# The second gate unit as twelve-bit parts, with the embedding's products moved between the two gate units

## What is computed

```python
x = layer_norm(ALPHA * x + mix, ln2_g[i], ln2_b[i])
ple = jax.nn.sigmoid(x @ w_ple_gate[i]) * (p[i] @ w_ple[i])
x = layer_norm(ALPHA * x + 0.5 * swiglu(x, ffn2_up[i], ffn2_down[i]) + ple, ln3_g[i], ln3_b[i])
```

## Time and profile before

| | |
|---|---|
| median of 3 runs | 2663.27 us (2658.33 to 2663.58) |
| profiled execution, its own time | 2664.31 us |
| span of it | 2662.6 us |
| mean granted TensorE clock | 0.997 |
| PE busy | 2624.8 us, 99% |
| DVE busy | 1116.0 us, 42% |
| ACT busy | 676.8 us, 25% |

### The profile page before, as it was taken

How to read it: one execution, slowest core, us unless ns; L and a number is a source line. 1 busy time by engine, 2 the same in 40 slices (tenths; PEclk the granted TensorE clock), 3 DMA queues, 4 the chain that set the end, 5 groups by cost and what they waited for, 6 DMA issues and landing times.

```text
span 2662.6 us, 38037 instructions
## 1 busy us (share of the span) xinstructions
PE 2624.8 (99%) x15353; PEld 1916.1 (72%) x15353; DVE 1116.0 (42%) x1589; ACT 676.8 (25%) x1202; POOL 73.4 (3%) x95
## 2 busy tenths in 40 slices
PE   8999999999999999999999999999999999999998
PEld 8989888999999998899989888843333333333333
DVE  6866424586587563157832143321212112112212
ACT  3414220342143042213412043021212121112111
POOL 0010200000000120000001000000000000000000
PEclk9999999999999999999999999999999999999999
DMA  7575334356655843334562644689999999999999
GB/s 240 189 271 182 125 127 164 137 177 221 234 176 186 293 166 117 136 143 159 173 215 90 225 151 158 248 352 427 428 427 428 428 428 428 427 427 427 427 427 411
DMA packets 265217, 705.27 MB, mean 265 GB/s; under 512 B 13076, under 2 KB 155360, under 8 KB 215072
## 3 DMA queue, kind: packets, MB, share of 16 engines
q1 hardware_dynamic: 253520, 663.66, 64.7%
q0 software_dynamic: 9856, 36.41, 3.8%
q10 hardware_dynamic: 1744, 3.83, 0.5%
HBM read 699.61 MB, written 6.60 MB: 265 GB/s over the span
## 4 chain that ended last, share of the span: by engine, by line
PE 82%; DMA 9%; SPq 8%; issue 1%; DVE 1%; ACT 0%; DVEq 0%
PE acc L989 12%; PE acc L1086 11%; PE acc L1708 9%; PE acc L1043 6%; PE mix L1047 6%; PE acc L1045 6%; SPq L871 5%; PE acc L1723 4%; PE acc L1528 4%; PE mix L1037 4%; PE acc L1015 3%; DMA big<-in_w 3%; SPq L874 2%; PE acc L1320 2%; DMA ring<-in_w 2%; DMA zp<-in_w 2%
## 5 line engine op out<-in xcount | busy, mean ns | idle before, releaser
L1043 PE MATMUL acc<-branch_parts,area_parts 128*128 128x256 f32 x1176 | 345.1, 293 | 4.4 <-DVE zz_parts L2360 4.3
L1047 PE MATMUL mix<-big_parts,zz_parts 128*128 128x256 f32 x1176 | 333.7, 284 | 0.0
L1045 PE MATMUL acc<-area_parts,ring_parts 128*128 128x256 f32 x1176 | 333.4, 284 | 0.0
L1086 PE MATMUL acc<-big,ring 128*128 128x256 f32 (+1 forms) x1408 | 269.7, 353 | 0.0
L1086 PEld LDWEIGHTS acc<-big,ring 128*128 128x128 f32 x1408 | 241.1, 190 | 28.3 <-issue 0.8
L3018 DVE COPY zz<-acc 128x512 f32<-128x512 f32 x32 | 22.1, 691 | 548.9 <-PE acc L1708 548.9
L1043 PEld LDWEIGHTS acc<-branch_parts,area_parts 128*128 128x128 f32 x1176 | 226.0, 192 | 13.6 <-DVE zz_parts L2360 5.2
L1045 PEld LDWEIGHTS acc<-area_parts,ring_parts 128*128 128x128 f32 x1176 | 226.1, 192 | 0.2
L1047 PEld LDWEIGHTS mix<-big_parts,zz_parts 128*128 128x128 f32 x1176 | 226.0, 192 | 0.0
L989 PE MATMUL acc<-x,ring 128*128 128x256 f32 x1024 | 224.3, 380 | 0.0
L989 PEld LDWEIGHTS acc<-x,ring 128*128 128x128 f32 x1024 | 193.8, 190 | 26.7 <-issue 0.3
(11 more groups left out here) (519 smaller groups left out, 3813.8 us busy)
## 6 DMA issues: line engine op xcount, KB each, us to landing
big<-in_w SPq DMA_DIRECT2D x89, 1024.0 KB, 25.9
ring<-in_ffn_up SPq DMA_DIRECT2D x86, 1024.0 KB, 5.0
ring<-in_w SPq DMA_DIRECT2D x84, 1024.0 KB, 25.9
ring<-in_w_in SPq DMA_DIRECT2D x72, 1024.0 KB, 7.1
spare<-in_w SPq DMA_DIRECT2D x42, 1024.0 KB, 25.9
area<-in_w_ada POOLq DMA_DIRECT2D x24, 1024.0 KB, 8.5
tables<-in_w SPq DMA_DIRECT2D x23, 1024.0 KB, 25.9
branch<-in_w SPq DMA_DIRECT2D x23, 1024.0 KB, 25.4
```

Source lines behind the costliest of these rows:

```text
L1043: pe.matmul(abank(a, b)[:, ts], wg[:, b, k, c * P:c * P + P], xg[:, k, :], start=c == 0 and k == 0, stop=False, skip_group_check=True)
L1045: pe.matmul(abank(a, b)[:, ts], wl[:, k, c0:c0 + P], xl[:, k, :], start=False, stop=k == K - 1, skip_group_check=True)
L1047: mm = pe.matmul(kbank(a, b)[:, ts], wk[:, b, k, c * P:c * P + P], xk[:, k, :], start=False, stop=k == K - 1, skip_group_check=True)
L1086: mm = pe.matmul(outs[c], w[:, k, c * P:c * P + P], rhs(kk), start=opens[c] and kk == 0, stop=kk == FC - 1, skip_group_check=not all(opens))
```

## The change

The second gate unit is multiplied by parts and not in the plain way, and is moved behind the embedding's products. It is counted as unit -1 of the second feed-forward (`split_unit(1, -1)`). The groups are renumbered: PLEG 39, PLE 40 and 41, the second gate unit (`G_PLEG_1`) 42. The embedding's second group is first copied into `res` by DVE and multiplied by the sigmoid later, as one instruction of 1024 elements.

```diff
             def split_product(L, s, u, i=0):
-                if s == 2:
+                whole = s == 2 or u == -1
+                if whole:
                     unit_landed(pe, L, r)
...
                 product_halves(L, PLEG, G_PLEG, cols, 32, between=lambda: half_stats(L, 1, 1, 4, 8))
-                product(L, PLEG + 1, G_PLEG + 1, xs, cols)
                 pe.wait_ge(apart_landed, (L + 1) * 48)
                 for hf in range(2):
                     a = G_PLE + hf
...
+                split_product(L, 1, -1)
                 ffn(L, UP2, G_UP2, 2)
```

On ACT:

```diff
-                for n in range(2):
-                    a = G_PLEG + n
-                    for b in range(2):
-                        bank_done(act, L, a, b)
-                        g = act.activation(big[:, 4 * n + 2 * b:4 * n + 2 * b + 2, :],
-                                           abank(a, b).rearrange("p (c t) -> p c t", c=2), ACT.Sigmoid)
-                    g.then_inc(acc_free[a % 2], 1)
-                    act.drain().then_inc(ple_gate, 1)
-                    if n == 0:
-                        for hf in range(2):
-                            upper(L, 1, 0, hf)
+                for hf in range(2):
+                    upper(L, 1, -1, hf)
+                a = G_PLEG
+                for b in range(2):
+                    bank_done(act, L, a, b)
+                    g = act.activation(big[:, 2 * b:2 * b + 2, :], abank(a, b).rearrange("p (c t) -> p c t", c=2), ACT.Sigmoid)
+                g.then_inc(acc_free[a % 2], 1)
+                act.drain().then_inc(ple_gate, 1)
+                a = G_PLEG_1
+                for b in range(2):
+                    bank_done(act, L, a, b)
+                    copy(big[:, 4 + 2 * b:6 + 2 * b, :], kbank(a, b).rearrange("p (c t) -> p c t", c=2)).then_inc(k_summed, 1)
+                    upper(L, 1, 0, b)
+                for b in range(2):
+                    act.wait_ge(a_joined, 26 * L + 13 + b + 1)
+                    act.activation(big[:, 4 + 2 * b:6 + 2 * b, :], big[:, 4 + 2 * b:6 + 2 * b, :], ACT.Sigmoid)
+                act.drain().then_inc(ple_gate, 1)
```

On DVE:

```diff
                 for hf in range(2):
-                    lower(L, 1, 0, hf)
+                    lower(L, 1, -1, hf)
+                v.wait_ge(ple_gate, L * 2 + 1)
                 for n in range(2):
                     a = G_PLE + n
-                    v.wait_ge(ple_gate, L * 2 + (n + 1))
                     for b in range(2):
                         bank_done(v, L, a, b)
                         m = 4 * n + 2 * b
-                        o = tt(res[:, m:m + 2, :], pair(abank(a, b)), big[:, m:m + 2, :], ALU.mult)
+                        o = tt(res[:, m:m + 2, :], pair(abank(a, b)), big[:, m:m + 2, :], ALU.mult) if n == 0 else \
+                            v.tensor_copy(res[:, m:m + 2, :], pair(abank(a, b)))
                     o.then_inc(acc_free[a % 2], 1)
+                for b in range(2):
+                    o = join(L, 1, -1, b, big[:, 4 + 2 * b:6 + 2 * b, :])
+                    if b:
+                        o.then_inc(acc_free[G_PLEG_1 % 2], 1)
+                    v.drain().then_inc(a_joined, 1)
+                    lower(L, 1, 0, b)
+                v.wait_ge(ple_gate, L * 2 + 2)
+                tt(res[:, 4:8, :], res[:, 4:8, :], big[:, 4:8, :], ALU.mult)
                 v.drain()
                 v.scalar_tensor_tensor(out=res[:, :, :], in0=res[:, :, :], scalar=1 / ALPHA, in1=x[:, :, :],
                                        op0=ALU.mult, op1=ALU.add)
```

More of the change, by code:

```diff
@@ L42 @@
 UP1, DOWN1, PROJ, GATE, MERGE, WOUT, PLEG, PLE, UP2, DOWN2, UNITS = 0, 11, 19, 24, 32, 34, 36, 38, 39, 50, 58
-G_UP1, G_DOWN1, G_PROJ, G_GATE, G_MERGE, G_WOUT, G_PLEG, G_PLE, G_UP2, G_DOWN2, GROUPS = \
-    0, 11, 15, 21, 29, 37, 39, 41, 43, 54, 58
+G_UP1, G_DOWN1, G_PROJ, G_GATE, G_MERGE, G_WOUT, G_PLEG, G_PLE, G_PLEG_1, G_UP2, G_DOWN2, GROUPS = \
+    0, 11, 15, 21, 29, 37, 39, 40, 42, 43, 54, 58
 ORDER = (0, 2, 3, 1)
@@ L675, in parts_made @@
         def parts_made(L, s):
-            return 56 * L + (0, 32, 22)[s]
+            return 58 * L + (0, 32, 22)[s]
         def half_parts(L, s, n, b):
-            return parts_made(L, s) + (2 * n + b + 3 if s == 1 else 2 * n + b + 1)
+            return parts_made(L, s) + (2 * n + b + 5 if s == 1 else 2 * n + b + 1)
         def sums_made(L, s):
-            return 50 * L + (0, 28, 20)[s]
+            return 52 * L + (0, 28, 20)[s]
         UPS = ((UP1, G_UP1), (UP2, G_UP2))
         def split_unit(s, n):
+            if (s, n) == (1, -1):
+                return PLEG + 1
             return UPS[s][0] + n if s < 2 else (PROJ + n if n < 4 else GATE)
         def split_group(s, n):
+            if (s, n) == (1, -1):
+                return G_PLEG_1
             return UPS[s][1] + n if s < 2 else (G_PROJ + n if n < 4 else G_GATE)
@@ L1028, in split_product @@
                 w, wl = (m[:, turn_of(L, r) % 2, :].rearrange("p (k c) -> p k c", c=UC) for m in (ring, ring_parts))
-                if s == 2:
+                whole = s == 2 or u == -1
+                if whole:
                     unit_landed(pe, L, r)
                 for b in range(2):
-                    if s < 2:
+                    if not whole:
                         half_landed(pe, L, r, b, i)
@@ L1856, in upper @@
             def upper(L, s, n, hf):
-                if s == 2:
+                if s == 2 or n == -1:
                     unit_landed(act, L, split_unit(s, n))
@@ L1892, in silus @@
                         upper(L, s, n + 1, 0)
-                    act.wait_ge(a_joined, 24 * L + (13 + n + 1 if s else n))
+                    act.wait_ge(a_joined, 26 * L + (15 + n + 1 if s else n))
                     act.activation(silu[:, a % 2], joined[0], ACT.Silu).then_inc(silu_ready, 1)
@@ L1969, in _ @@
                 k_sum(2, 1, rg)
-                act.wait_ge(a_joined, 24 * L + 10 + 1)
+                act.wait_ge(a_joined, 26 * L + 10 + 1)
                 act.activation(rg, rg, ACT.Silu)
@@ L1981, in _ @@
                 for b in range(2):
-                    act.wait_ge(a_joined, 24 * L + 11 + b + 1)
+                    act.wait_ge(a_joined, 26 * L + 11 + b + 1)
                     act.activation(big[:, 2 * b:2 * b + 2, :], big[:, 2 * b:2 * b + 2, :], ACT.Sigmoid)
@@ L2379, in join @@
                 bank_done(v, L, a, b)
-                v.wait_ge(k_summed, sums_made(L, s) + (2 * n + b + 1 if s == 1 else 2 * n + b - 1))
+                v.wait_ge(k_summed, sums_made(L, s) + (2 * n + b + 3 if s == 1 else 2 * n + b - 1))
                 return v.scalar_tensor_tensor(out=dst, in0=abank(a, b).rearrange("p (c t) -> p c t", c=2), scalar=1.0 + 1.0 / STEP,
```

## The result

The changed kernel took 2670.48 us (median of 7 runs, 2669.60 to 2675.28), the kernel before in the same rounds 2661.58 us (7 runs, 2658.33 to 2663.58). The ratio is 1.0033, with a 95% interval of 1.0023 to 1.0043: slower by 8.9 us. The forecast was 2672.5, or 9.2 us above the median that was known then.

A forecast was written before the change was run, and what follows sets the result against it. PE, busy 99% of the span, was taken to bound the kernel. The terms -4.0 + 6.6 + 4.4 + 2.8 = +9.8 us gave 2673.1 by the median; the forecast was 2672.5, range 2665.5 to 2678.5.

The forecast's parts named there:

- The product by parts, -4.0: On PE's list, 64 plain matmuls (13.81 us) give way to a unit of 11.79 us: -2.02 us per layer, twice.
- rival 5: The second gate unit is held up inside by its parts, so PE's list is not shorter: 2677 us, chance 0.03.
- The first wait, +6.6: At the second gate unit's opening PE waits for DVE to read the embedding's first bank pair: 3.1 and 3.5 us.
- The second wait, +4.4: At UP2's first parts PE waits for DVE, whose product and merge precede the join: 2.2 us per layer.
- The clock, +2.8: Granted clock falls in PE's wait at the second gate unit's opening, 1.4 us per layer; nothing counted at UP2.
- first rival: The granted clock does not fall at PE's new waits: +7.0 us, 2670.3 us, chance 0.17.
- second rival: Either the read of the embedding's first pair or the merge hides: 2.5 to 5 us slower, some 2667.5, chance 0.08.
- the other side: DVE's conversions, reads and merge are ready in time, PE's list decides: 4.0 us gained, 2659.2 us, chance 0.07.
- fourth rival: After PE's wait at UP2 the clock falls too, or joins stay late: another 3 to 6 us, some 2679, chance 0.10.

The follow-up runs named there:

- the repetition: The changed kernel run once more, unaltered, beside the later runs on their chip: 2675.27 us, ratio 1.0041 against the kernel before.
- the late merge: Changed kernel with the 1024-element product and the merge of res with x moved behind the second feed-forward's joins: 2668.34 us, ratio 1.0022.
- the early read: Changed kernel with DVE reading the embedding's first two banks between the two halves of the gate unit's conversions: 2664.52 us, ratio 1.0007.
- the two runs with extra products: Changed kernel with 13 or 6 float32 products added between the embedding and the second gate unit: 2674.94 us and 2669.13 us.
- the filled wait: Changed kernel with 6 float32 products (12 matmul instructions) between the embedding and the second gate unit: 2669.13 us, ratio 1.0027.
- the two single edits: Changed kernel with either the embedding's first banks read earlier or the merge of res with x done later: 2664.52 us and 2668.34 us.
- the version with both edits: Changed kernel with the embedding's first banks read earlier and the merge done later: 2659.32 us, ratio 0.9985; run again 2660.47 us, ratio 0.9994.

## Why the prediction was right

**The product by parts, -4.0.** Right: the stage without waits is 2.02 us shorter in each layer. This also answers rival 5.

**The first wait, +6.6.** The mechanism was right (the same two engines, the same two instructions), the size a little too large: 2.9 us from the embedding's end to the opening in each layer, and 0.1 us for the first matmuls after a pause, 6.0 in all. I had given the second layer 3.5 us, because x's conversion ended 0.86 us behind the first gate unit there. In the changed kernel it is 0.49 in both (1207.89 against 1207.40 in the second), and 0.5 in both layers of the eight other profiles: what I took for a feature of the layer was seen in the one profile of the kernel before and in no other.

**The second wait, +4.4.** Right: the bank takes 8.07 us in place of 5.90, 2.17 a layer. The chain on DVE came out as reckoned (product and merge end 16.0 us after the gate unit's bank 0).

**The clock, +2.8.** That the clock falls at these waits and what one fall costs came out right; how often it falls and when did not. I set 1.4 us for each of the two first waits and nothing for the second, since near the start of the kernel the clock had fallen 2.0 us after PE stopped, and I expected the lower level from inside the first waits on. The stretches above show 1.00 through the waits; in the five falls of the two profiles of the changed kernel the lower level began 0.3 to 1.5 us after PE had resumed. Measured, a fall costs 1.5 us, where 1.4 was two thirds of a row, a guess that luck brought close. Whether a fall comes changes from run to run, behind the second kind of wait as well: in the profiles that have them, 4 of 6 first waits (two each of the changed kernel, its repetition and the late merge) and 3 of 10 second waits (two each of the changed kernel, its repetition, the early read and the two runs with extra products) had a fall. One fall in the first profile, four in the repetition: 1.5 and 6.0 us.

By stages that makes -4.0 + 6.0 + 4.3 + 1.6 = +7.9 in the profile of 2670.01 us and +12.3 in that of 2676.07 us. The forecast's +9.8 lies between them, and so does the measured 8.9. That 2672.5 came within 2.0 us of the median is luck in part: two terms of the sum are right by their mechanism, but the clock's moves with the execution, and the five runs of the repetition had their median at 2675.27 us.

**The rivals.** That the clock holds (first rival) is the case with the filled wait, +6.3 us by the stages; in the changed kernel it never was seen in all four places. That one wait is covered (second rival) is what the two single edits made of it. That neither DVE's reads nor the merge hold PE up (the other side) is true of the version with both edits and of no other. Of the fourth rival one half failed and one half came in some executions: behind the second wait the banks follow at 5.90 us again, so the joins do not stay late, but the clock did fall there in both layers of the repetition, for another 3.0 us.

The Trainium skill's limit for an idle gap ("TensorE: Matmul & The Clock Gate", section "HAM oscillation — how this bites in real kernels") would have kept the clock up in all of these waits. The trace disagrees: the granted clock was at its lower level behind waits of 2.9 and even of 2.1 us. The measurement decides.

## What to carry to other kernels

On an engine that runs without a gap, a shorter instruction list is worth its difference only if every buffer that it opens is free by then: before moving a product, list what stands ahead of the instruction that frees its buffer on the other engine's list. Here DVE was busy for 42% of the span, and still its order cost three times what the products saved, while two changes of that order removed the loss and, by the stages, gave the 4.0 us (by the runs 3.4 and 1.75, the second not told from nothing). Waits of 2 to 3 us on TensorE should be priced with the clock's fall behind them, here 1.5 us in 7 of 16 such waits, which by the profiles also makes single runs of the same kernel differ by several us.

## What was not expected

- A fall of the granted clock was seen behind waits of 2.1 us (bank of 9.56 in place of 8.07 us), not only behind the 4.3 us of the earlier trace rows, and both outcomes occur in the same program at the same instruction: 7.55 and 6.00 us in the two layers of one execution.
- With twelve extra matmul instructions in the first wait, the profile shows no fall there in either layer, and they cost nothing: the gate unit opened 22.32 us and 22.33 us after the stage's start, against 22.32 and 22.31 without them. That the products prevent the fall is likely but not shown beyond chance. Where PE was kept at work, with 6 or 13 products, there was no fall in 4 of 4 places, against 4 falls in 6 where it idled; but in the same two profiles the second waits, which were not filled, had no fall either.
